# Last feed-forward stage of a two-block model on 256 columns instead of 272, with each input's high and low parts as one moving operand

## The chip, the cores and the metric

The kernel runs on one core of one Trainium2 chip. The metric is the device time of one execution in microseconds (us), the median of several runs. TensorE (PE in the rows) does the matmuls, VectorE is DVE, ScalarE is ACT, GpSimd is POOL, and SyncE (SP) issues the weight loads. PSUM is eight banks of 128 partitions by 512 fp32 values, named `bank0` to `bank7`.

## The reference, cut to what matters

Two blocks in a row. The first one puts 16 meta tokens ahead of 256 tokens and has two layers of feed-forward, mixer, feed-forward:

```python
h = jnp.concatenate([meta, x], axis=1)            # 16 + 256 rows of 1024
for l in range(DEPTH):                            # DEPTH = 2
    h = h + 0.5 * swiglu(rmsnorm(h, norm_gains[l, 0]), ...)
    h = h + mixer(rmsnorm(h, norm_gains[l, 1]), ...)
    h = h + 0.5 * swiglu(rmsnorm(h, norm_gains[l, 2]), ...)
return rmsnorm(h, final_norm)[:, N_META:]         # the 16 meta rows are dropped

def swiglu(x, w_gate, w_up, w_down):              # 1024 -> 2816 -> 1024
    return (jax.nn.silu(x @ w_gate) * (x @ w_up)) @ w_down
```

The second block (a short convolution, two mixtures of 64 experts, a sparse attention) works on the 256 tokens that are left. Everything is float32.

## The kernel before, in words

Activations lie transposed: features on the 128 partitions, rows of the sequence along the free dimension, the 256 tokens first and the 16 meta tokens behind them (`T` = 272, `SEQ` = 256). `H` is the residual in `KD` = 8 feature tiles. One stage is one of the reference's lines; the last feed-forward stage, `ffn(1, 1)`, is the subject here.

**Split products.** A feed-forward product is made of fp32r matmuls (a rounded form of fp32 that TensorE takes at one pass). Input and weights are each cut in a rounded high part and a rounded rest, the low part, and three products are summed in PSUM: low weights by high input, high weights by low input, high weights by high input. `split_sum` (matmuls at L528) does so for one *chunk* of weights, which is all `k` tiles of one 128-column output tile: 8 tiles for gate and up, 11 for half of a down product. `SQ` holds the input's high part and `XN` its low part; for the down products `HIDH` and `HID` (in `ARENA`) do.

**Who makes the parts.** The weights come by DMA into three ring buffers. ACT copies a chunk to its high part, rounded (`high_part`, L1057), and POOL subtracts that from the weights and leaves the low part (`low_parts`, L1758). High parts have room for `HIGHS` = 3 chunks, so `high_part` of chunk c waits until TensorE has finished chunk c - 3, and TensorE's chunk c waits for POOL's low part of it (`wl_ready`).

**The order of the work** is written out by hand for each engine, and each engine takes its instructions in that order. For each of the 22 hidden tiles `f`, TensorE makes chunk 2f (gate) in bank 0 or 2 and chunk 2f+1 (up) in bank 1 or 3; from f = 2 on it first waits for `hid_ready` of tile f - 2, which frees the banks. ACT does `Silu` of the gate bank into `SG` (L1097), and behind it the high parts of chunks 2f+3 and 2f+4:

```python
st.need(bank_full["act"][pair])
st.done(A(SG[:, f % 2, :], bank[pair][:, 0:T], ACT.Silu), silu_ready)
high_part()
high_part()
```

DVE waits for the silu and the up bank, multiplies them twice, once in fp32 (L1369) and once rounded into `HIDH` (L1370), and subtracts for the low part in `HID` (L1371, two inputs in SBUF), which gives `hid_ready`. Then come 16 down chunks in 8 banks; DVE adds half of each bank to `H` (L1376), and ACT squares `H` for the next norm (L1062). A norm is a matmul of the squares with a constant (L560), ACT's square root (L1072), DVE's reciprocal (L1328) and a chain of scaling (L1331), rounding (ACT, L1067) and subtracting (L1335). `then(...)` is an instruction of DVE and a wait for its own result.

The rows below also draw on two other stages with split products: the mixer's last part, where DVE does L1494 to L1499, and the convolution, where it does L1520 to L1529, both while POOL makes low parts. Lines L498 and L492 are the mixer's plain fp32 products, each of which leaves two records.

Of the kernel before, what the change touches and what calls it, by code (L numbers as in the profile page):

```python
# [7 lines left out]
ALU = mybir.AluOpType  # L8
# [6 lines left out]
P = 128  # L15
# [279 lines left out]
def build_model(nc, w, cst_dram, small_dram, h0_dram, table_dram, out_dram):  # L295
    CL, SL = const_layout(), small_layout()
    with ExitStack() as ctx:
        twins = {}

        def sb(name, shape, dt=F32, twin=False):  # L300
            if twin:
                with nc.sbuf_tensor(name + "_rounded", shape, F32R) as t:
                    twins[name] = t
            return ctx.enter_context(nc.sbuf_tensor(name, shape, dt))

        def rounded(view):
# [60 lines left out]
        sq_ready = sem("sq_ready")  # L367
        std_ready = sem("std_ready")
        xn_ready = sem("xn_ready")
        silu_ready = sem("silu_ready")  # L370
# [104 lines left out]
        def _(pe):  # L475
# [41 lines left out]
            def split_sum(o, tiles, start=True, stop=True, before=None, cols=slice(0, P), again=False):  # L517
# [12 lines left out]
                                               stop=(stop and k == len(tiles) - 1 and j == 2))  # L530
                return ins

            def chunk_done(ins, s):
# [13 lines left out]
            def rows(x, n=T):  # L547

                return [x[:, k, 0:n] for k in range(KD)]

            def pairs(high, low, n, m=T):

                return [(high[:, k, 0:m], low[:, k, 0:m]) for k in range(n)]

            def column_means(b, wgt, tiles, reader):

                claim(b)
                for k, x in enumerate(tiles):
# [5 lines left out]
            def rms_norm():  # L564
                column_means(7, "mean_d", rows(SQ), "act")

            def layer_norm(b):

# [8 lines left out]
                st.need(x_tile, KD)  # L577

            def ffn(l, j):
                rms_norm()  # L580
                tiles = pairs(SQ, XN, KD)
                for f in range(NF):
                    pair = 2 * (f % 2)
                    if f >= 2:
                        st.need(hid_ready)
                    for m, e in ((0, "act"), (1, "dve")):
                        claim(pair + m)
                        ins = split_sum(bank[pair + m][:, 0:T], tiles,
                                        before=(lambda k: st.need(xn_ready)) if f == 0 and m == 0 else None)
                        chunk_done(ins, bank_full[e][pair + m])  # L590
                tiles = pairs(HIDH, HID, NF)
                for c in range(4):
                    for h in range(2):
                        for dt in range(2):
                            b = (4 if c % 2 == 0 else 0) + dt
                            if h == 0:
                                claim(b)
                            last_hidden = lambda f: st.need(hid_ready) if f >= 9 else None
                            ins = split_sum(bank[b][:, 0:T], tiles[h * 11:h * 11 + 11], start=(h == 0), stop=(h == 1),
                                            before=last_hidden if (c, h, dt) == (0, 1, 0) else None)  # L600
# [415 lines left out]
            for l in range(2):  # L1016
                ffn(l, 0)
                mixer(l)
                ffn(l, 1)
            rms_norm()  # L1020
            convolution()
            layer_norm(0)
            experts(0)
# [8 lines left out]
        def _(act):  # L1032
# [41 lines left out]
            def rms_norm(first=False):  # L1074
                if first:
                    for k in range(KD):
                        square(k, True)
                deviation(RS[:, :], 7, "eps_rms", T, std_ready)

            def layer_norm(b):  # L1080
                st.need(d2a)
# [4 lines left out]
            def ffn(first=False, dense_next=False):  # L1086
                rms_norm(first)
                split_input(XN)
# [197 lines left out]
            for l in range(2):  # L1286
                ffn(first=(l == 0))
                mixer(l)
                ffn(dense_next=True)
            rms_norm()  # L1290
            convolution()
            layer_norm(0)
            experts(0)
# [8 lines left out]
        def _(dve):  # L1302
# [54 lines left out]
            def sum_from(b, k):  # L1357
# [2 lines left out]
                st.done(STT(R2[:, k, :], X2[:, k, :], ALPHA, bank[b][:, 0:SEQ], ALU.mult, ALU.add), sum_tile)  # L1360
                mark(bank_free["dve"][b])

            def ffn(l, j):
                normed_and_split("gains", (l * 3 + 2 * j) * KD, XN, xn_ready)
                for f in range(NF):
                    b = 2 * (f % 2) + 1
                    st.need(silu_ready)
                    st.need(bank_full["dve"][b])
                    st.done(TT(HID[:, f, :], SG[:, f % 2, :], bank[b][:, 0:T], ALU.mult))  # L1369
                    then(TT(rounded(HIDH[:, f, :]), SG[:, f % 2, :], bank[b][:, 0:T], ALU.mult))  # L1370
                    st.done(TT(rounded(HID[:, f, :]), HID[:, f, :], part(HIDH[:, f, :]), ALU.subtract), hid_ready)  # L1371
                for c in range(4):
                    for dt in range(2):
                        b, k = (4 if c % 2 == 0 else 0) + dt, 2 * c + dt
                        st.need(bank_full["dve"][b])
                        st.done(STT(H[:, k, :], bank[b][:, 0:T], 0.5, H[:, k, :], ALU.mult, ALU.add), h_tile)  # L1376
                        mark(bank_free["dve"][b])
# [538 lines left out]
```

## Time and profile before

| | us |
|---|---|
| median of 3 runs | 3162.02 |
| lowest and highest | 3161.73, 3163.46 |
| span of the profiled execution, first to last instruction | 3154.3 |
| what lies around the span, against the median | 7.7 |
| PE busy | 2718.0 (86%), 18120 matmul records |
| DVE, ACT, POOL busy | 920.7, 911.3, 890.8 (28 to 29% each) |
| split products of `ffn(1, 1)` on the chain | 197.03 |

The profile is of one execution, whose only time is its span. An engine's busy share is an average over all stages. What one stage is worth is read from the stage: from the rows of its own window, in order of time, and from what each engine waited for there.

### The profile page before, as it was taken

How to read it: one execution, taken by the hardware profiler on the slowest of the kernel's cores; microseconds unless marked ns; L12 is line 12 of the kernel's file. 1: busy time of each engine (PE TensorE's matmuls, PEld its weight loads, DVE VectorE, ACT ScalarE, POOL GpSimd, SP SyncE). 2: the span in 40 equal slices, each digit the busy share in tenths (PEclk: the TensorE clock that was granted, in tenths of full speed). 3: DMA queues.
4: the chain of work that ended last, by engine and by line, in shares of the span. 5: the costliest groups of instructions: out<-in, count | busy, mean ns of one | idle time of the engine just before them, and what ended most of it. 6: DMA issues, size and time to landing. Idle time of an engine off the chain costs nothing.

```text
span 3154.3 us, 44882 instructions
## 1 busy us (share of the span) xinstructions
PE 2718.0 (86%) x18120; PEld 2044.0 (65%) x18120; DVE 920.7 (29%) x2251; ACT 911.3 (29%) x1485; POOL 890.8 (28%) x374
## 2 busy tenths in 40 slices
PE   5999997899999999789987888888877769888886
PEld 3997666799999656789986433333366754334333
DVE  2211523521220243432164322222225343222222
ACT  3331361333433145133332111111124411111111
POOL 2882001578677001257863000000024500000000
PEclk8999996999999999699997899999978979999998
DMA  6543320354555322045455799999943169999994
GB/s 168 187 156 114 107 81 27 107 178 152 166 179 159 119 80 81 5 156 178 152 161 196 256 366 367 367 366 366 312 151 107 31 204 366 366 366 367 367 366 165
DMA packets 515163, 643.89 MB, mean 204 GB/s; under 512 B 16544, under 2 KB 450720, under 8 KB 514768
## 3 DMA queue, kind: packets, MB, share of 16 engines
q1 hardware_dynamic: 513424, 635.60, 60.2%
q0 software_dynamic: 1600, 6.29, 0.9%
q8 instruction: 104, 1.70, 0.2%
q14 instruction: 35, 0.29, 0.0%
HBM read 637.66 MB, written 4.19 MB: 203 GB/s over the span
## 4 chain that ended last, share of the span: by engine, by line
PE 62%; SPq 21%; DVE 8%; DMA 5%; issue 2%; ACT 2%; POOL 0%; DVEq 0%; ACTq 0%
PE bank L528 33%; PE bank L492 14%; SPq L1805 10%; SPq L1801 10%; DMA wring<-in_exp_w 4%; PE bank L983 3%; PE bank L778 2%; PE bank L944 2%; PE bank L968 1%; PE bank L560 1%; PE bank L695 1%; PE bank L957 1%; PE bank L502 1%; PE bank L991 1%; DMA bias_table<-ARENA 1%
## 5 line engine op out<-in xcount | busy, mean ns | idle before, releaser
L1758 POOL TENSOR_TENSOR wring_rounded<-wring,wring_rounded 128x1024 fp32r<-128x1024 f32 (+1 forms) x336 | 861.1, 2566 | 477.1 <-ACT wring_rounded L1057 454.1
L528 PE MATMUL bank<-SQ_rounded,wring_rounded 128*128 128x272 f32 (+1 forms) x3456 | 659.6, 291 | 45.0 <-POOL wring_rounded L1758 23.9
L528 PEld LDWEIGHTS bank<-SQ_rounded,wring_rounded 128*128 128x128 f32 x3456 | 550.6, 191 | 49.6 <-issue 38.4
L1057 ACT ACTIVATE wring_rounded<-wring 128x1024 fp32r<-128x1024 f32 (+1 forms) x336 | 375.1, 1119 | 489.9 <-PE bank L528 484.9
L528 PE MATMUL bank<-XN_rounded,wring_rounded 128*128 128x272 f32 (+1 forms) x1728 | 500.2, 289 | 0.0
L528 PE MATMUL bank<-ARENA_rounded,wring_rounded 128*128 128x272 f32 (+1 forms) x3456 | 447.8, 293 | 54.0 <-DVE ARENA_rounded L1489 27.6
L528 PEld LDWEIGHTS bank<-ARENA_rounded,wring_rounded 128*128 128x128 f32 x3456 | 444.9, 194 | 57.0 <-DVE ARENA_rounded L1489 28.5
L983 PE MATMUL bank<-wring,ARENA 128*32 128x512 f32 x2048 | 281.1, 672 | 139.1 <-DMA wring<-in_exp_w 108.8
L528 PEld LDWEIGHTS bank<-XN_rounded,wring_rounded 128*128 128x128 f32 x1728 | 331.7, 192 | 0.0
L1272 ACT ACTIVATE ARENA<-bank 128x512 f32<-128x512 f32 x128 | 76.4, 597 | 794.7 <-PE bank L983 794.7
L492 PE MATMUL bank<-XN,wring 128*128 128x272 f32 (+2 forms) x1088 | 257.1, 401 | 11.8 <-DVE XN L1342 11.8
L983 PEld LDWEIGHTS bank<-wring,ARENA 128*32 128x32 f32 x2048 | 57.5, 116 | 308.7 <-DMA wring<-in_exp_w 164.8
L968 PE MATMUL bank<-ARENA 64*128 64x512 f32 x1008 | 250.4, 615 | 0.0
L492 PEld LDWEIGHTS bank<-XN,wring 128*128 128x128 f32 (+2 forms) x1088 | 190.2, 180 | 68.1 <-DVE XN L1342 12.6
L991 PEld LDWEIGHTS bank<-CST,ARENA 128*128 128x128 f32 x1024 | 124.4, 192 | 117.2 <-ACT ARENA L1272 117.2
L1784 POOL DMA_DIRECT2D ARENA<-bias_table x8 | 6.0, 754 | 621.4 <-DVE H L1354 621.4
L1369 DVE TENSOR_TENSOR ARENA<-ARENA,bank 128x272 f32<-128x272 f32 x88 | 38.6, 438 | 430.8 <-PE bank L528 430.8
L944 PE MATMUL bank<-ARENA 128*128 128x128 f32 x1024 | 136.1, 288 | 32.0 <-DVE ARENA L1703 27.9
L1717 DVE TENSOR_TENSOR ARENA<-ARENA,bank 128x64 f32<-128x64 f32 x128 | 28.4, 222 | 462.4 <-ACT ARENA L1277 462.4
L944 PEld LDWEIGHTS bank<-ARENA 128*128 128x128 f32 x1024 | 123.5, 197 | 61.5 <-DVE ARENA L1703 34.2
L1767 POOL TENSOR_TENSOR ARENA_rounded<-ARENA,ARENA_rounded 128x256 fp32r<-128x256 f32 (+1 forms) x24 | 17.7, 737 | 498.6 <-ACTq L1039 498.6
L957 PE MATMUL bank<-ARENA 128*32 128x512 f32 x1024 | 143.2, 632 | 7.9 <-issue 7.9
(231 smaller groups left out, 2475.2 us busy)
## 6 DMA issues: line engine op xcount, KB each, us to landing
wring<-in_exp_w SPq DMA_DIRECT2D x256, 1024.0 KB, 11.7
ARENA<-in_exp_w SPq DMA_DIRECT2D x128, 1024.0 KB, 12.4
wring<-in_ffn_w_gate SPq DMA_DIRECT2D x44, 1024.0 KB, 5.3
wring<-in_ffn_w_up SPq DMA_DIRECT2D x44, 1024.0 KB, 7.9
wring<-in_ffn_w_down SPq DMA_DIRECT2D x32, 1408.0 KB, 6.3
wring<-in_w_in SPq DMA_DIRECT2D x16, 2048.0 KB, 7.7
wring<-in_conv_w_in SPq DMA_DIRECT2D x24, 512.0 KB, 5.4
wring<-in_attn_w_in SPq DMA_DIRECT2D x5, 2048.0 KB, 7.9
```

Source lines behind the costliest of these rows:

```text
L492: ins = nc.tensor.matmul(o, l, r, start=(i == 0), stop=(i == len(g) - 1))
L528: ins = nc.tensor.matmul(o, rounded(a_[:, k, cols]), rounded(x), start=(start and k == 0 and j == 0), stop=(stop and k == len(tiles) - 1 a ...
L944: ins = nc.tensor.matmul(GATHER[:, kk * P:(kk + 1) * P], XTOK[:, t, k * P:(k + 1) * P], GS[:, t, :], start=(t == 0), stop=(t == 1))
L957: ins = nc.tensor.matmul(DOWN[32 * q:32 * q + 32, :], HT[:, c * 32:c * 32 + 32], w2[:, c, dh * 512:dh * 512 + 512], start=True, stop=True, ...
L968: ins = nc.tensor.matmul(bank[2 * t + dh][:, :], PUT[64 * dh:64 * dh + 64, u % 2, t * P:(t + 1) * P], YS[64 * dh:64 * dh + 64, :], start=f ...
L983: ins = nc.tensor.matmul(UP[32 * q:32 * q + 32, :], XG[:, k, u * 32:u * 32 + 32], v[:, k, :], start=(k < 4), stop=(k >= 4), tile_position= ...
L991: ins = nc.tensor.matmul(TURN[:, f * 32:f * 32 + 32], HS[:, f * P:(f + 1) * P], const("sum4"), start=True, stop=True)
L1057: st.done(A(rounded(high), w_, ACT.Copy), wh_ready)
L1272: A(HS[:, :], UP[:, :], ACT.Copy).then_inc(m.hs, 1)
L1758: st.done(nc.gpsimd.tensor_tensor(rounded(low), low, part(high), ALU.subtract), wl_ready)
L1801: sp.dma_start(v[:, :, j, :], w[name][l][bass.ds(e, 1)].rearrange("o (k p) n -> p (o k) n", p=P)).then_inc(M[l].w13[u], 16)
L1805: sp.dma_start(W2B[:, u, :].rearrange("p (k n) -> p k n", k=2), w["exp_w2_2"][l][bass.ds(e, 1)].rearrange("o (k p) n -> p (o k) n", p=P)). ...
```

## The change

Only the stage `ffn(1, 1)` and the norm behind it change. They work on the 256 tokens alone. `XN` and `SQ` become the two halves of one tile `XS`, so that a moving operand of 2 x 256 columns can take the high part and the low part in one instruction. For each `k`, the new `wide_sum` issues two matmuls for the former three: the high weights by high and low input (512 columns, the whole bank), and the low weights by the high input (256 columns, onto the bank's first half). What was one sum of 272 columns is now two partial sums of 256 columns in one bank, and DVE adds them: for the gate ahead of the silu, which ACT then does in place on `SG`, for the up product ahead of the multiplication, and for the down product by adding both halves to `H` in turn.

```diff
+        def both(high, low):
+            ap = [list(x) for x in high.ap]
+            return bass.AP(tensor=twins[high.tensor.name], offset=high.offset,
+                           ap=[ap[0], [low.offset - high.offset, 2], ap[1]])
...
-        XN = sb("XN", [P, KD, T], twin=True)
-        SQ = sb("SQ", [P, KD, T], twin=True)
+        XS = sb("XS", [P, 2, KD, T], twin=True)
+        SQ, XN = XS[:, 0], XS[:, 1]
...
+            def wide_sum(o, tiles, start=True, stop=True, before=None):
...
+                pe.wait_ge(wl_ready, c + 1)
+                for k, (xh, xl) in enumerate(tiles):
+                    if before:
+                        before(k)
+                    nc.tensor.matmul(o[:, 0:2 * SEQ], rounded(high[:, k, :]), both(xh, xl),
+                                     start=(start and k == 0), stop=False, skip_group_check=True)
+                    ins = nc.tensor.matmul(o[:, 0:SEQ], rounded(low[:, k, :]), rounded(xh),
+                                           start=False, stop=(stop and k == len(tiles) - 1), skip_group_check=True)
...
-                    for m, e in ((0, "act"), (1, "dve")):
+                    for m, e in ((0, "act" if n == T else "dve"), (1, "dve")):
...
-                    st.need(bank_full["act"][pair])
-                    st.done(A(SG[:, f % 2, :], bank[pair][:, 0:T], ACT.Silu), silu_ready)
+                    if n == T:
+                        st.need(bank_full["act"][pair])
+                        st.done(A(SG[:, f % 2, :], bank[pair][:, 0:T], ACT.Silu), silu_ready)
+                    else:
+                        st.need(gate_ready)
+                        st.done(A(SG[:, f % 2, 0:n], SG[:, f % 2, 0:n], ACT.Silu), silu_ready)
...
+            def ffn_of_tokens(gain, at):
+                normed_and_split(gain, at, XN, xn_ready, SEQ)
+                for f in range(NF):
+                    g, u = bank[2 * (f % 2)], bank[2 * (f % 2) + 1]
+                    sg, hid, high = SG[:, f % 2, 0:SEQ], HID[:, f, 0:SEQ], HIDH[:, f, 0:SEQ]
+                    st.need(bank_full["dve"][2 * (f % 2)])
+                    then(v.tensor_copy(sg, g[:, 0:SEQ]))
+                    st.done(TT(sg, sg, g[:, SEQ:2 * SEQ], ALU.add), gate_ready)
+                    st.need(bank_full["dve"][2 * (f % 2) + 1])
+                    then(v.tensor_copy(hid, u[:, 0:SEQ]))
+                    then(TT(hid, hid, u[:, SEQ:2 * SEQ], ALU.add))
+                    st.need(silu_ready)
+                    st.done(TT(hid, sg, hid, ALU.mult))
+                    st.settle()
+                    then(v.tensor_copy(rounded(high), hid))
+                    st.done(TT(rounded(hid), hid, part(high), ALU.subtract), hid_ready)
+                for c in range(4):
+                    for dt in range(2):
...
+                        then(STT(h, bank[b][:, 0:SEQ], 0.5, h, ALU.mult, ALU.add))
+                        st.done(STT(h, bank[b][:, SEQ:2 * SEQ], 0.5, h, ALU.mult, ALU.add), h_tile)
+                        mark(bank_free["dve"][b])
```

What DVE does for two hidden tiles of this stage, before (L1369 to L1371, three instructions a tile):

```order
L1369 TENSOR_TENSOR ARENA<-ARENA,bank 128x272
L1370 TENSOR_TENSOR ARENA_rounded<-ARENA,bank 128x272
L1371 TENSOR_TENSOR ARENA_rounded<-ARENA,ARENA_rounded 128x272
L1369 TENSOR_TENSOR ARENA<-ARENA,bank 128x272
L1370 TENSOR_TENSOR ARENA_rounded<-ARENA,bank 128x272
L1371 TENSOR_TENSOR ARENA_rounded<-ARENA,ARENA_rounded 128x272
```

and in the changed kernel, for one hidden tile and the start of the next:

```order
L1398 COPY ARENA<-bank 128x256
L1399 TENSOR_TENSOR ARENA<-ARENA,bank 128x256
L1401 COPY ARENA<-bank 128x256
L1402 TENSOR_TENSOR ARENA<-ARENA,bank 128x256
L1404 TENSOR_TENSOR ARENA<-ARENA 128x256
L1406 CAST ARENA_rounded<-ARENA 128x256
L1407 TENSOR_TENSOR ARENA_rounded<-ARENA,ARENA_rounded 128x256
L1398 COPY ARENA<-bank 128x256
```

Three instructions of a tile have become seven. One of the old three read SBUF alone; of the new seven the last three do. The sum of the next gate (L1398, L1399) stands behind them.

What ACT does for one hidden tile and the start of the next, from f = 2 on, with the semaphores that each waits for; before:

```order
L1097 ACTIVATE ARENA<-bank 128x272 [waits bank0_full_act,hid_ready]
L1057 ACTIVATE wring_rounded<-wring 128x1024 [waits bank0_full_act,w_ready0]
L1057 ACTIVATE wring_rounded<-wring 128x1024 [waits bank1_full_dve,w_ready1]
L1097 ACTIVATE ARENA<-bank 128x272 [waits bank2_full_act,hid_ready]
L1057 ACTIVATE wring_rounded<-wring 128x1024 [waits bank2_full_act,w_ready1]
```

and in the changed kernel:

```order
L1125 ACTIVATE ARENA<-ARENA 128x256 [waits gate_sum_ready,hid_ready]
L1081 ACTIVATE wring_rounded<-wring 128x1024 [waits bank0_full_dve,w_ready0]
L1081 ACTIVATE wring_rounded<-wring 128x1024 [waits bank1_full_dve,w_ready1]
L1125 ACTIVATE ARENA<-ARENA 128x256 [waits gate_sum_ready,hid_ready]
L1081 ACTIVATE wring_rounded<-wring 128x1024 [waits bank2_full_dve,w_ready1]
```

The silu waited for TensorE's gate bank; it now waits for DVE's sum of the gate, and the two high parts stand behind it as before.

## Rows read from the trace of the kernel before

**Rows 1.** The page's chain that ended last, by engine
```profile
PE 62%; SPq 21%; DVE 8%; DMA 5%; issue 2%; ACT 2%; POOL 0%; DVEq 0%; ACTq 0%
```

**Rows 2.** The same chain in order of time: start, us, what
```profile
1386.56 197.03 PE bank L528 x1566
1583.59 3.68 PE bank L560 x16
```

**Rows 3.** Two stretches: PE, PEld, DVE, ACT, POOL busy, clock, DMA share, GB/s
```profile
1386.50:1518.50 132.00, 131.94 (x1051) 131.78 (x1052) 27.50 (x68) 55.36 (x68) 104.33 (x43) 1.00 0.48 150
1518.50:1583.50 65.00, 65.00 (x518) 65.00 (x517) 4.02 (x8) 22.04 (x22) 50.74 (x17) 1.00 0.61 182
```

**Rows 4.** Timeline of one hidden tile of `ffn(1, 1)`: start, us, instruction, idle before
```profile
1451.02 1.06 ACT L1057 ACTIVATE wring_rounded<-wring 128x1024 fp32r<-128x1024 f32 x1 [1.66 <-PE bank L528]
1451.03 0.44 DVE L1369 TENSOR_TENSOR ARENA<-ARENA,bank 128x272 f32<-128x272 f32 x1 [4.75 <-PE bank L528]
1451.85 0.44 DVE L1371 TENSOR_TENSOR ARENA_rounded<-ARENA,ARENA_rounded 128x272 fp32r<-128x272 f32 x1
1452.15 2.40 POOL L1758 TENSOR_TENSOR wring_rounded<-wring,wring_rounded 128x1024 fp32r<-128x1024 f32 x1 [0.32 <-ACT wring_rounded L1057]
1454.02 0.40 ACT L1097 ACTIVATE ARENA<-bank 128x272 f32<-128x272 f32 x1 [1.95 <-PE bank L528]
1454.32 1.05 ACT L1057 ACTIVATE wring_rounded<-wring 128x1024 fp32r<-128x1024 f32 x1
1455.44 2.41 POOL L1758 TENSOR_TENSOR wring_rounded<-wring,wring_rounded 128x1024 fp32r<-128x1024 f32 x1 [0.89 <-ACT wring_rounded L1057]
1457.04 0.44 DVE L1369 TENSOR_TENSOR ARENA<-ARENA,bank 128x272 f32<-128x272 f32 x1 [4.75 <-PE bank L528]
```

**Rows 5.** Timeline of the down chunks of the same stage, POOL
```profile
1543.57 3.22 POOL L1758 TENSOR_TENSOR wring_rounded<-wring,wring_rounded 128x1408 fp32r<-128x1408 f32 x1 [0.93 <-ACT wring_rounded L1057]
1547.73 3.22 POOL L1758 TENSOR_TENSOR wring_rounded<-wring,wring_rounded 128x1408 fp32r<-128x1408 f32 x1 [0.94 <-ACT wring_rounded L1057]
```

**Rows 6.** Timeline of other products: convolution, its output product, fp32 of 272 columns
```profile
1602.05 0.40 PE L528 MATMUL bank<-SQ_rounded,wring_rounded 128*128 128x256 f32 x2
1602.40 0.40 PE L528 MATMUL bank<-SQ_rounded,wring_rounded 128*128 128x256 f32 x2
...
1680.94 2.41 POOL L1758 TENSOR_TENSOR wring_rounded<-wring,wring_rounded 128x1024 fp32r<-128x1024 f32 x1 [0.29 <-ACT wring_rounded L1057]
1683.67 2.41 POOL L1758 TENSOR_TENSOR wring_rounded<-wring,wring_rounded 128x1024 fp32r<-128x1024 f32 x1 [0.31 <-ACT wring_rounded L1057]
...
310.76 0.40 ACT L1126 ACTIVATE SQ<-bank 128x272 f32<-128x272 f32 x1 [3.27 <-PE bank L492]
314.43 0.40 ACT L1126 ACTIVATE SQ<-bank 128x272 f32<-128x272 f32 x1 [3.27 <-PE bank L492]
```

**Rows 7.** Timeline of the mixer's last part: DVE beside POOL
```profile
1318.10 0.45 DVE L1499 TENSOR_TENSOR ARENA_rounded<-ARENA,ARENA_rounded 128x272 fp32r<-128x272 f32 x1
1318.27 2.53 POOL L1758 TENSOR_TENSOR wring_rounded<-wring,wring_rounded 128x1024 fp32r<-128x1024 f32 x1 [0.83 <-ACT wring_rounded L1057]
1318.81 0.43 DVE L1496 TENSOR_TENSOR ARENA<-ARENA,bank 128x272 f32<-128x272 f32 x1
1319.28 1.81 DVE L1497 TENSOR_TENSOR ARENA<-ARENA 128x272 f32<-128x272 f32 x1
1321.12 0.30 DVE L1498 CAST ARENA_rounded<-ARENA 128x272 fp32r<-128x272 f32 x1
```

**Rows 8.** Timeline of the convolution: a DVE instruction with one SBUF tensor beside POOL
```profile
1603.00 4.81 POOL L1758 TENSOR_TENSOR wring_rounded<-wring,wring_rounded 128x1024 fp32r<-128x1024 f32 x2 [15.83 <-ACT wring_rounded L1057]
...
1604.82 0.73 DVE L1523 TENSOR_SCALAR ARENA<-ARENA,SM 128x256 f32<-128x256 f32 x1 [0.18 <-DVE ARENA L1520]
```

**Rows 9.** Instruction groups of the attention: DVE copies out of PSUM, busy and mean ns
```profile
L1449 DVE COPY ARENA<-bank 128x256 f32<-128x256 f32 x16 | 6.6, 412 | 2.8 <-PE bank L502 2.8
```

**Rows 10.** A stretch of the mixer's last part: PE busy, clock, DMA share, GB/s
```profile
1325.00:1330.00 5.00, 2.23 (x11) 0.78 0.00 0
```

More of the change, by code:

```diff
@@ L369, in build_model @@
         xn_ready = sem("xn_ready")
-        silu_ready = sem("silu_ready")
+        silu_ready, gate_ready = sem("silu_ready"), sem("gate_sum_ready")
         hid_ready = sem("hid_ready")
@@ L531, in split_sum @@
                 return ins
+            def wide_sum(o, tiles, start=True, stop=True, before=None):
+                progress["chunk"] += 1
+                c = progress["chunk"] - 1
+                low, high = chunk_views(c)
+                pe.wait_ge(wl_ready, c + 1)
[6 more added lines that the diff above has]
+                                           start=False, stop=(stop and k == len(tiles) - 1), skip_group_check=True)
+                return ins
             def chunk_done(ins, s):
@@ L562, in column_means, with rms_norm @@
                 st.done(ins, bank_full[reader][b])
-            def rms_norm():
-                column_means(7, "mean_d", rows(SQ), "act")
+            def rms_norm(n=T):
+                column_means(7, "mean_d", rows(SQ, n), "act")
             def layer_norm(b):
@@ L579, in ffn @@
             def ffn(l, j):
-                rms_norm()
-                tiles = pairs(SQ, XN, KD)
+                n = SEQ if (l, j) == (1, 1) else T
+                total = wide_sum if n == SEQ else split_sum
+                rms_norm(n)
+                tiles = pairs(SQ, XN, KD, n)
                 for f in range(NF):
@@ L585, in ffn @@
                         st.need(hid_ready)
-                    for m, e in ((0, "act"), (1, "dve")):
+                    for m, e in ((0, "act" if n == T else "dve"), (1, "dve")):
                         claim(pair + m)
-                        ins = split_sum(bank[pair + m][:, 0:T], tiles,
-                                        before=(lambda k: st.need(xn_ready)) if f == 0 and m == 0 else None)
+                        ins = total(bank[pair + m][:, 0:2 * SEQ if n == SEQ else T], tiles,
+                                    before=(lambda k: st.need(xn_ready)) if f == 0 and m == 0 else None)
                         chunk_done(ins, bank_full[e][pair + m])
-                tiles = pairs(HIDH, HID, NF)
+                tiles = pairs(HIDH, HID, NF, n)
                 for c in range(4):
@@ L598, in ffn @@
                             last_hidden = lambda f: st.need(hid_ready) if f >= 9 else None
-                            ins = split_sum(bank[b][:, 0:T], tiles[h * 11:h * 11 + 11], start=(h == 0), stop=(h == 1),
-                                            before=last_hidden if (c, h, dt) == (0, 1, 0) else None)
+                            ins = total(bank[b][:, 0:2 * SEQ if n == SEQ else T], tiles[h * 11:h * 11 + 11],
+                                        start=(h == 0), stop=(h == 1),
+                                        before=last_hidden if (c, h, dt) == (0, 1, 0) else None)
                             if h == 1:
@@ L1019, in _ @@
                 ffn(l, 1)
-            rms_norm()
+            rms_norm(SEQ)
             convolution()
@@ L1072, in deviation, with rms_norm @@
                 st.done(A(out, bank[b][:, 0:n], ACT.Sqrt, bias=const(eps)), s)
-            def rms_norm(first=False):
+            def rms_norm(first=False, n=T):
                 if first:
@@ L1077, in rms_norm @@
                         square(k, True)
-                deviation(RS[:, :], 7, "eps_rms", T, std_ready)
+                deviation(RS[:, 0:n], 7, "eps_rms", n, std_ready)
             def layer_norm(b):
@@ L1084, in layer_norm, with ffn @@
                 deviation(RS[:, 0:SEQ], b + 1, "eps_ln", SEQ, std_ready)
-            def ffn(first=False, dense_next=False):
-                rms_norm(first)
-                split_input(XN)
+            def ffn(first=False, dense_next=False, n=T):
+                rms_norm(first, n)
+                split_input(XN, n)
                 if first:
@@ L1288, in _ @@
                 mixer(l)
-                ffn(dense_next=True)
-            rms_norm()
+                ffn(dense_next=True, n=SEQ if l == 1 else T)
+            rms_norm(n=SEQ)
             convolution()
@@ L1361, in sum_from @@
                 mark(bank_free["dve"][b])
+            def ffn_of_tokens(gain, at):
[16 more added lines that the diff above has]
+                    for dt in range(2):
+                        b, k = (4 if c % 2 == 0 else 0) + dt, 2 * c + dt
+                        h = H[:, k, 0:SEQ]
+                        st.need(bank_full["dve"][b])
+                        then(STT(h, bank[b][:, 0:SEQ], 0.5, h, ALU.mult, ALU.add))
+                        st.done(STT(h, bank[b][:, SEQ:2 * SEQ], 0.5, h, ALU.mult, ALU.add), h_tile)
+                        mark(bank_free["dve"][b])
             def ffn(l, j):
+                if (l, j) == (1, 1):
+                    ffn_of_tokens("gains", (l * 3 + 2 * j) * KD)
+                    return
                 normed_and_split("gains", (l * 3 + 2 * j) * KD, XN, xn_ready)
```

## The prediction

> **What bounds the kernel now.** I read the chain of waits first: TensorE holds 62% of it, DVE 8%, POOL next to nothing [rows 1]. In order of time, the split products of the last feed-forward stage are one piece of 197.03 us in which TensorE waits for nothing, and the mean of the next norm follows at once [rows 2]. The stretches of the stage say the same: PE busy throughout at full clock, ACT under half busy, DVE a fifth, but POOL 104.33 of 132 us while gate and up are made and 50.74 of 65 in the down part [rows 3]. So the stage is bound by the pace of its matmuls, and POOL is the engine with the least room.
>
> A hidden tile takes 6.01 us, the distance of two L1369 [rows 4], for 48 matmuls: 125.2 ns each, 113.3 of them for 272 columns at 2.4 GHz. A down chunk takes 4.16 us for 33 [rows 5]: 126 ns. The columns are nearly the whole price.
>
> **What the matmuls save.** Three times 272 columns (816) become 512 + 256 (768), and three weight loads two. What comes on top of the columns differs: 12 ns a matmul in this stage; 12 in the convolution, where three matmuls of 256 columns take 0.35 to 0.36 us against 0.32 of columns; 7 in its output product, where 24 take 2.73 us, 113.5 each [rows 6]. No fp32r matmul of 512 columns is in the trace. The nearest long one is a plain fp32 record of 272 columns: 3.67 us for 16, 229 ns each, 226.7 of them two passes over the columns [rows 6], so 2.5 on top. Bounds for a pair: 320 ns of columns + 2.5 + 12 = 335 if the excess shrinks for the long one, and 356 if it is a share of the columns (11%). I take 345, 12 for each load, near the middle. The saving is 31 ns a pair. Gate and up have 22 x 2 x 8 = 352 pairs (a chunk 3.01 -> 2.76 us), down has 16 x 11 = 176 (4.16 -> 3.80). TensorE alone would save 11 + 5.8 us.
>
> The TensorE page of the Trainium skill ("Back-to-back issue gap") gives 2.5 ns over the columns per matmul, so 325 ns a pair, an estimate from that page; the rows of this stage disagree with it at 12 ns for the short ones and agree for the long one.
>
> **What DVE gets.** Seven instructions a tile for three. Copy from PSUM 0.41 us [rows 9], additions with a PSUM operand 0.43 [rows 7], some 0.04 between dependent ones (0.42 for 256 columns). Gate sum 0.87, up sum 0.91 with its wait, product 0.42, cast 0.29, subtraction 0.42: about 3 us of 5.5. By length that fits. By its neighbours it may not.
>
> **The wait that appears.** In the mixer, L1497 (both inputs in SBUF) takes 1.81 us instead of 0.44 and ends 0.29 after POOL's L1758; L1496, with a PSUM input, takes 0.43 in the middle of the same POOL instruction; and a POOL instruction that starts 0.17 after L1499 takes 2.53 instead of 2.40 [rows 7]. So a DVE instruction on SBUF alone and POOL's subtraction exclude each other: whoever starts first runs, the other waits. POOL lets go some 0.14 before its record ends, DVE 0.28 after its start. L1523, with a single SBUF tensor, also waits for the first of two POOL instructions (0.73 us) [rows 8]. Before, a hidden tile had one such instruction, and L1371 fell into POOL's pause from 1451.83 to 1452.15 [rows 4]. Now it has three, product, cast and subtraction, and POOL's two take 4.8 of 5.5 us. They must meet.
>
> The cast is the open one: L1498 took 0.30, but no POOL instruction was running [rows 7]. The SBUF page of the Trainium skill ("Who interferes with whom") says that copies and casts between SBUF can also take the pair of ports that DVE shares with GpSimd. No run so far shows it for the cast; L1523 is the nearest row, and I let the cast wait as it does.
>
> **What is queued behind it.** DVE's gate sum of f+1 stands behind the subtraction of f; ACT's silu waits for that sum; behind the silu stands the high part of chunk 2f+5, the up chunk of f+2; POOL waits for it, TensorE for POOL. Going round this loop with the durations above, every second tile is hit fully:
> - TensorE up(f): 2.76
> - up sum on DVE: 0.99 with the hand-over; the POOL instruction that began 0.26 before the up chunk's end lets go at 2.00, and the product ends at 2.42
> - POOL's next instruction was queued and has the port before the cast asks: the cast ends 2.41 later
> - subtraction: 0.46; altogether 5.29 from the up chunk
> - gate sum f+1: 0.80; silu: 0.43; high part with hand-over: 1.03 [rows 4]
> - POOL 2.40, hand-over 0.07, and TensorE may start up(f+2).
>
> That is 12.78 us for two tiles: 6.39 each against 6.01, although TensorE needs 5.52. It stands idle 1.74 us once in two tiles. In the odd tile product and cast slip through and only the subtraction waits. A pair price of 335 or 356 moves this by nothing, since the up chunk then starts when POOL says. If the cast does not wait, it takes 0.33 for 2.41, but the subtraction is then caught, 2.2 for 0.46: 5.0 for 5.29, and the two tiles take 12.45, 6.23 each.
>
> **The sum.** Gate and up: the first two tiles run on the three chunks made ahead at 5.5 (-1.0), twenty at +0.38 (+7.6): +6.6. Entry to the down part: the second down chunk's high part stands behind the last silu, which comes 1.8 after the last up chunk (its gate sum stands behind a subtraction that POOL held up); 1.35 for the high part and 3.4 for the low one make 6.6, and TensorE ends the first down chunk at 3.8: it waits 2.8, where it waited 0. Down: 16 x 0.36 = -5.8; POOL's 3.22 and ACT's 1.38 stay under 3.80, and DVE's second addition to `H` reads PSUM and excludes nobody. Edges: two means on 256 columns, 3.68 -> 3.5 us each [rows 2], and a norm chain of some 8.5 us on a seventeenth fewer columns: -0.8 (bounds 0 and -1). The second addition of the last bank (+0.44) lies beside ACT's high part of 1.06 and costs nothing there. The second mean, 3.68 us long, covers it. Loads: the 150 GB/s of gate and up stay about as they are and the down part's 182 become 200 [rows 3]; TensorE never waited for them and the buffers are three deep, so no cost. Sum: 6.6 + 2.8 - 5.8 - 0.8 = **+2.8 us**: a span of 3157.1, and a median of 3164.8, since the median stands 7.7 above the span. By bounds: pair 335, cast free: -2.6; pair 356, POOL holding to its record's end (+0.2 a tile): +9.
>
> A measurement of this kernel can tell some 0.2%, 6.3 us, from no change. So I forecast no change that can be told: TensorE's saving is real and is handed to the port.
>
> **Rivals.**
> 1. *Exclusion does not bite.* DVE's three fall into pauses as L1371 does, or PE's pace keeps the engines in step. For it: before, all of it fell in step, for 22 tiles. Against: 0.7 us of pause a tile cannot hold three instructions and their waits. It would give -11 - 5.8 - 0.8 = -17.6: 3144.4. Chance 0.13. With half of the tiles in step: 3151 to 3156, chance 0.08.
> 2. *One blocked wait more in the loop* (the slower side). If the product of the odd tile is also caught, or the hand-overs are 0.1 us longer, so that POOL's queued instruction wins once more, two tiles cost 2.4 more: 15.2. Over ten double tiles +24: 3189; for half of them 3177. It decides when the odd up sum ends after POOL's start instead of 0.6 before it, and that is a margin of half a microsecond. Chance 0.15.
> 3. *The clock falls.* TensorE is idle 1.74 us in 12.8. In the mixer a stretch with over half idle shows 0.78 [rows 10], a mix of the 1.2 and 2.4 GHz levels. Here the busy share is 86%, so I do not expect it; once a loop would cost about 1 us of matmul each: +10, 3175. Chance 0.06.
> 4. *The pairs cost what the triples did* (376 ns; a long moving operand of two pieces costs extra, or the excess grows). Gate and up go by POOL and DVE, down saves nothing: 3171. Chance 0.05.
>
> **Chances and range.** The forecast (0.53) spans -2.6 to +9, of it 0.45 within 6.3 us and 0.07 above, 0.01 below. Faster: 0.13 + 0.07 of rival 1 + 0.01 = 0.21. Slower: 0.07 + 0.15 + 0.06 + 0.05 = 0.33. Same: 0.46. The range from 3150 to 3182 takes in the half-in-step case, the clock, the dear pairs and half of rival 2, and leaves out some 0.2; the likeliest case's own is 3159 to 3171.
>
> **What would show it.** In the changed kernel's timeline of one hidden tile: products, casts or subtractions of 1.5 to 2.5 us that end 0.3 behind POOL's record; TensorE waiting for POOL or its queue once in two tiles, and pieces of the chain of waits that name POOL, ACT and DVE where there were none; a gate and up stretch of 137 to 141 us and a down stretch near 62. Down chunks at 3.68 or 3.92 us would correct the pair price. I am wrong if gate and up run at 5.5 us a tile, or if the casts always take 0.29 with POOL running.

## The result, and the profile after

Over 20 runs each, the changed kernel takes 3168.09 us (median; 3161.24 to 3170.53) and the kernel before 3163.44 (3156.56 to 3166.55). The ratio is 1.0015, with a 95% interval of 1.0008 to 1.0022: 4.7 us slower, 2.5 to 7.0 by the interval. That is no change by the 0.2% of the prediction, but the interval leaves out zero: over 20 runs each it is a small loss.

The two profiled spans differ by more, 3154.3 and 3164.4. The norm's mean ahead of the stage and the one behind it frame the part that was changed. The chain of the kernel before, in order of time (start, us, what):

```profile
1374.10 3.95 PE bank L560 x16
...
1583.59 3.68 PE bank L560 x16
```

and of the changed kernel:

```profile
1380.66 3.73 PE bank L581 x16
...
1594.31 0.24 PE bank L548
1595.01 3.47 PE bank L581 x16
```

From mean to mean it is 209.5 us before and 214.4 after: 4.9 more, close to the measured 4.7. Of the 10.1 us between the spans another 6.6 are there when the stage begins, in code that the change leaves alone, and 1.3 come back behind it. Nor is the profiled execution of the kernel before a typical one. Wherever a time and its span are both on record, the time is 1.8 or 1.9 us above the span; so by my estimate the execution with the span of 3154.3 took about 3156.1, some 6 us less than the median of before. I compare stages by the distance from mean to mean from here on, since it is free of that.

The new waits of the changed kernel, from the stage's window (engine, line, who was waited for: us in total, times, longest):

```profile
ACT ARENA L1125 <- DVE ARENA L1399: 80.3, 22, 5.3
POOL wring_rounded L1815 <- ACT wring_rounded L1081: 51.4, 23, 12.5
DVE ARENA L1401 <- PE bank L550: 23.0, 11, 2.1
PE bank L548 <- POOL wring_rounded L1815: 15.9, 11, 2.4
```

Before, TensorE waited for nothing in 197 us [rows 2]. Now it waits 11 times for POOL, 15.9 us in all: ten times once in two hidden tiles, 1.3 to 1.4 us each, and 2.4 us at the entry to the down part. And the silu waits for DVE's gate sum 22 times. DVE's own instructions say why (busy, mean ns, idle before):

```profile
L1407 DVE TENSOR_TENSOR ARENA_rounded<-ARENA,ARENA_rounded 128x256 fp32r<-128x256 f32 x22 | 30.8, 1401 | 0.8
L1406 DVE CAST ARENA_rounded<-ARENA 128x256 fp32r<-128x256 f32 x22 | 30.2, 1372 | 0.8
L1404 DVE TENSOR_TENSOR ARENA<-ARENA 128x256 f32<-128x256 f32 x22 | 18.2, 826 | 0.8
L1402 DVE TENSOR_TENSOR ARENA<-ARENA,bank 128x256 f32<-128x256 f32 x22 | 9.3, 422 | 0.8
```

The three that touch SBUF alone take 1401, 1372 and 826 ns on average, where their lengths are 420, 300 and 420; the one with a PSUM operand takes its 422. Those are 54 us of waiting that the record counts as busy.

One turn of the loop, two hidden tiles, from the timeline of the changed kernel:

```profile
1434.69 4.94 POOL L1815 TENSOR_TENSOR wring_rounded<-wring,wring_rounded 128x1024 fp32r<-128x1024 f32 x2
1436.17 1.20 DVE L1404 TENSOR_TENSOR ARENA<-ARENA 128x256 f32<-128x256 f32 x1
1437.40 2.37 DVE L1406 CAST ARENA_rounded<-ARENA 128x256 fp32r<-128x256 f32 x1
1439.81 0.43 DVE L1407 TENSOR_TENSOR ARENA_rounded<-ARENA,ARENA_rounded 128x256 fp32r<-128x256 f32 x1
1440.15 0.42 DVE L1398 COPY ARENA<-bank 128x256 f32<-128x256 f32 x1
1440.60 0.42 DVE L1399 TENSOR_TENSOR ARENA<-ARENA,bank 128x256 f32<-128x256 f32 x1
1441.11 0.42 ACT L1125 ACTIVATE ARENA<-ARENA 128x256 f32<-128x256 f32 x1 [4.74 <-DVE ARENA L1399]
1441.44 2.00 ACT L1081 ACTIVATE wring_rounded<-wring 128x1024 fp32r<-128x1024 f32 x2
1441.85 0.43 DVE L1404 TENSOR_TENSOR ARENA<-ARENA 128x256 f32<-128x256 f32 x1
1442.31 0.30 DVE L1406 CAST ARENA_rounded<-ARENA 128x256 fp32r<-128x256 f32 x1
1442.56 9.94 POOL L1815 TENSOR_TENSOR wring_rounded<-wring,wring_rounded 128x1024 fp32r<-128x1024 f32 x4 [2.94 <-ACT wring_rounded L1081]
1442.64 2.58 DVE L1407 TENSOR_TENSOR ARENA_rounded<-ARENA,ARENA_rounded 128x256 fp32r<-128x256 f32 x1
...
1449.02 1.22 DVE L1404 TENSOR_TENSOR ARENA<-ARENA 128x256 f32<-128x256 f32 x1
```

In the first tile the product waits for POOL's running instruction (1.20), the cast for its next one (2.37). Behind them stand the gate sum (L1398, L1399), the silu, two high parts, and POOL, which stood idle for 2.94 us meanwhile. In the second tile product and cast slip through (0.43, 0.30), the subtraction does not (2.58). POOL is held up by DVE too, for less: its 44 instructions of this length take 2.40 us on average before and 2.48 now; the pair of 4.94 us is one of 2.40 and one of 2.57, which starts while the product has not ended. The turn takes 1449.02 - 1436.17 = 12.85 us, 6.43 a tile, against 6.01 before [rows 4].

The price of the pair, first while the hidden tiles are made (TensorE's records) and then in the down part (DVE's first reading of a finished bank; one down chunk lies between the two):

```profile
1448.61 0.40 PE L548 MATMUL bank<-XS_rounded,wring_rounded 128*128 128x512 f32 x1
1448.84 0.28 PE L550 MATMUL bank<-XS_rounded,wring_rounded 128*128 128x256 f32 x1
1448.96 0.40 PE L548 MATMUL bank<-XS_rounded,wring_rounded 128*128 128x512 f32 x1
...
1450.72 0.40 PE L548 MATMUL bank<-XS_rounded,wring_rounded 128*128 128x512 f32 x1
```

```profile
1545.14 0.42 DVE L1413 SCALAR_TENSOR_TENSOR H<-bank,H 128x256 f32<-128x256 f32 x1 [11.13 <-PE bank L550]
...
1548.99 0.42 DVE L1413 SCALAR_TENSOR_TENSOR H<-bank,H 128x256 f32<-128x256 f32 x1 [2.96 <-PE bank L550]
```

Six pairs from 1448.61 to 1450.72 are 352 ns each; eleven in 3.85 us are 350. A down chunk took 4.16 before [rows 5].

### The profile page after: what moved, and what is told of

It is laid out like the page before. It is cut to its first block, busy times and chain, and to the rows that moved or that the text cites. A ratio compares the mean times of both kernels' runs of the same rounds, so it can differ in the third digit from the quotient of the medians.

```text
span 3164.4 us, 43922 instructions
## 1 busy us (share of the span) xinstructions
PE 2709.5 (86%) x17592; PEld 2007.0 (63%) x17592; DVE 1008.6 (32%) x2347; ACT 910.6 (29%) x1485; POOL 892.4 (28%) x374
## 4 chain that ended last, share of the span: by engine, by line
PE 60%; SPq 18%; DVE 10%; DMA 6%; ACT 2%; issue 2%; POOL 1%; DVEq 0%; ACTq 0%
PE bank L534 27%; PE bank L498 14%; SPq L1862 9%; SPq L1858 9%; DMA wring<-in_exp_w 5%; PE bank L1007 3%; PE bank L548 2%; PE bank L968 2%; PE bank L802 2%; PE bank L992 2%; PE bank L581 1%; PE bank L981 1%; PE bank L719 1%; PE bank L508 1%; POOL wring_rounded L1815 1%
## 5 line engine op out<-in xcount | busy, mean ns | idle before, releaser
L534 PE MATMUL bank<-XS_rounded,wring_rounded 128*128 128x272 f32 (+1 forms) x4128 | 524.6, 290 | 41.8 <-POOL wring_rounded L1815 24.9
L534 PEld LDWEIGHTS bank<-XS_rounded,wring_rounded 128*128 128x128 f32 x4128 | 522.4, 192 | 45.2 <-issue 35.0
L534 PE MATMUL bank<-ARENA_rounded,wring_rounded 128*128 128x272 f32 (+1 forms) x2928 | 381.5, 294 | 55.6 <-DVE ARENA_rounded L1546 27.3
L534 PEld LDWEIGHTS bank<-ARENA_rounded,wring_rounded 128*128 128x128 f32 x2928 | 378.9, 195 | 58.7 <-DVE ARENA_rounded L1546 28.5
L498 PE MATMUL bank<-XS,wring 128*128 128x272 f32 (+2 forms) x1088 | 259.2, 404 | 11.8 <-DVE XS L1370 11.8
L498 PEld LDWEIGHTS bank<-XS,wring 128*128 128x128 f32 (+2 forms) x1088 | 191.0, 181 | 69.5 <-DVE XS L1370 12.6
L548 PE MATMUL bank<-XS_rounded,wring_rounded 128*128 128x512 f32 x352 | 127.6, 404 | 17.5 <-POOL wring_rounded L1815 13.5
L1015 PE MATMUL bank<-CST,ARENA 128*128 128x32 f32 x1024 | 138.0, 279 | 1.4 <-ACT ARENA L1300 1.4
L1426 DVE TENSOR_TENSOR ARENA<-ARENA,bank 128x272 f32<-128x272 f32 x66 | 28.9, 438 | 327.7 <-PE bank L534 327.7
```

The source lines that it names most:

```text
L498: ins = nc.tensor.matmul(o, l, r, start=(i == 0), stop=(i == len(g) - 1))
L534: ins = nc.tensor.matmul(o, rounded(a_[:, k, cols]), rounded(x), start=(start and k == 0 and j == 0), stop=(stop and k == len(tiles) - 1 a ...
L548: nc.tensor.matmul(o[:, 0:2 * SEQ], rounded(high[:, k, :]), both(xh, xl), start=(start and k == 0), stop=False, skip_group_check=True)
L1015: ins = nc.tensor.matmul(TURN[:, f * 32:f * 32 + 32], HS[:, f * P:(f + 1) * P], const("sum4"), start=True, stop=True)
```

## The experiments

The theory: the saving of TensorE is real, and is lost to a loop (product, cast and subtraction held up by POOL; gate sum behind them; silu; high part; POOL; TensorE). The rivals: that the port is simply full; that seven instructions of DVE are too long a chain; that the pairs cost about what the triples did.

**e1: cut the loop, leave the waits.** ACT makes one high part ahead of the silu and of the wait for `hid_ready` (cut to this stage; the other stages keep their order):

```diff
-                    if f >= 2:
+                    if f >= 2 and n == T:
                         st.need(hid_ready)
...
+                        high_part()
+                        if f >= 2:
+                            st.need(hid_ready)
                         st.need(gate_ready)
                         st.done(A(SG[:, f % 2, 0:n], SG[:, f % 2, 0:n], ACT.Silu), silu_ready)
-                    high_part()
+                    if n == T:
+                        high_part()
                     high_part()
```

> The changed kernel with one edit: ACT makes the high part of chunk 2f+3 ahead of the silu of tile f, not behind it; all arithmetic, all DVE instructions and all three waits for the port stay. Loop theory (the loss is the loop DVE sum, silu, high part, POOL, TensorE): the loop is cut, the pauses of TensorE go, a hidden tile takes 8 x 2 x 352 ns = 5.63 us, gate and up plus down take 22 x 5.63 + 16 x 3.85 = 186 us for 199 before, and with the shorter norms the kernel is some 14 us faster than before (ratio 0.9955). Capacity rival (POOL's 4.8 us and DVE's three port instructions of 0.3 do not fit in 5.63 us whatever the order): the tile stays near 6.2 to 6.4 and the kernel within 6 us of before or slower. DVE-length rival (seven instructions are too long a chain by themselves): no change against the changed kernel, ratio 1.0015.

Measured: 3145.01 us, ratio 0.9945 (0.9932 to 0.9959). From mean to mean it is 195.5 us, 14.0 less than before, and once its hidden tiles have begun TensorE waits for nobody. By the ratio the whole kernel is 17 us faster (13 to 21). The stage's 14.0 lie inside that; the rest lies outside the stage, in code that the edit leaves alone, and its cause stays open. DVE's groups in the stage, and the timeline of one tile:

```profile
L1410 DVE CAST ARENA_rounded<-ARENA 128x256 fp32r<-128x256 f32 x22 | 50.9, 2315 | 0.8
L1411 DVE TENSOR_TENSOR ARENA_rounded<-ARENA,ARENA_rounded 128x256 fp32r<-128x256 f32 x22 | 12.3, 558 | 0.8
L1408 DVE TENSOR_TENSOR ARENA<-ARENA 128x256 f32<-128x256 f32 x22 | 10.7, 487 | 0.8
```

```profile
1438.57 0.43 DVE L1408 TENSOR_TENSOR ARENA<-ARENA 128x256 f32<-128x256 f32 x1
1438.85 2.40 POOL L1819 TENSOR_TENSOR wring_rounded<-wring,wring_rounded 128x1024 fp32r<-128x1024 f32 x1 [0.35 <-ACT wring_rounded L1081]
1439.03 2.37 DVE L1410 CAST ARENA_rounded<-ARENA 128x256 fp32r<-128x256 f32 x1
...
1444.20 0.43 DVE L1408 TENSOR_TENSOR ARENA<-ARENA 128x256 f32<-128x256 f32 x1
```

A tile takes 1444.20 - 1438.57 = 5.63 us, TensorE's pace. The cast still waits, and takes 2315 ns on average for its 300: 49 us of waiting by the three groups, nearly the 54 of the changed kernel, and it costs nothing. So there is room for POOL's and DVE's work in 5.63 us (the capacity rival falls), the chain is not too long, and the pairs are cheaper than the triples. It was the order in which the waits stood.

**e2: leave the loop, take the waits away.** The silu goes to PSUM, and a second product takes the place of the cast:

```diff
-                        st.done(A(SG[:, f % 2, 0:n], SG[:, f % 2, 0:n], ACT.Silu), silu_ready)
+                        st.done(A(bank[6 + f % 2][:, 0:n], SG[:, f % 2, 0:n], ACT.Silu), silu_ready)
...
-                    st.done(TT(hid, sg, hid, ALU.mult))
-                    st.settle()
-                    then(v.tensor_copy(rounded(high), hid))
+                    act_sg = bank[6 + f % 2][:, 0:SEQ]
+                    st.done(TT(rounded(high), act_sg, hid, ALU.mult))
+                    then(TT(hid, act_sg, hid, ALU.mult))
```

> The changed kernel with the silu written to PSUM banks 6 and 7, so that both products read one operand there (a second product takes the place of the cast, as in the kernel before): still seven DVE instructions a tile, of the same lengths or longer (product 0.42 for cast 0.29), but only the subtraction needs the port. Exclusion theory: products take 0.42 us also beside POOL, at most one wait a tile remains, TensorE's pauses go, a tile takes 5.63 us and the kernel is some 14 us faster than before (0.9955). DVE-length rival: nothing changes or it gets 0.1 us a tile worse, ratio 1.0015 to 1.002.

Measured: 3145.49 us, ratio 0.9945 (0.9932 to 0.9959); 195.1 us from mean to mean. The products in its trace, with an operand in PSUM:

```profile
L1407 DVE TENSOR_TENSOR ARENA_rounded<-ARENA,ARENA_rounded 128x256 fp32r<-128x256 f32 x22 | 14.6, 662 | 0.7
L1405 DVE TENSOR_TENSOR ARENA_rounded<-bank,ARENA 128x256 fp32r<-128x256 f32 x22 | 9.3, 424 | 0.7
L1406 DVE TENSOR_TENSOR ARENA<-bank,ARENA 128x256 f32<-128x256 f32 x22 | 9.1, 415 | 0.0
```

424 and 415 ns, with POOL running beside them; only the subtraction still waits, 0.24 us on average. A tile takes 5.60 us. Seven instructions and the old order of ACT are harmless without the waits: the length rival falls. POOL's own work in the loop is as long as before here (2.49 us on average), so it was DVE's waits that made the loop too long.

**e3: shorten what is waited for.** POOL makes two of the 8 or 11 weight tiles of a low part in this stage, and the matmuls use those two in turn, so most of the low weights are left out:

```diff
                     pool.wait_ge(wh_ready, c + 1)
+                    if chunks[c][0][0] in ("up", "down") and chunks[c][0][1:3] == (1, 1):
+                        low, high = low[:, 0:2, :], high[:, 0:2, :]
...
-                    ins = nc.tensor.matmul(o[:, 0:SEQ], rounded(low[:, k, :]), rounded(xh),
+                    ins = nc.tensor.matmul(o[:, 0:SEQ], rounded(low[:, k % 2, :]), rounded(xh),
```

> The changed kernel in which POOL makes only the first two of 8 (or 11) weight tiles of each low part of the last feed-forward stage (0.6 to 0.75 us instead of 2.4 and 3.2), and the matmuls with the low weights use those two in turn: it leaves out most of the low weights. DVE's and ACT's work and order are unchanged. Exclusion theory: no wait above 0.7 us is left, a tile takes 5.63 us, kernel some 14 us faster than before (0.9955). DVE-length rival: as the changed kernel, 1.0015.

Measured: 3144.03 us, ratio 0.9943 (0.9929 to 0.9957); 194.9 us from mean to mean. POOL and the cast beside it, from the timeline:

```profile
1438.72 0.73 POOL L1817 TENSOR_TENSOR wring_rounded<-wring,wring_rounded 128x256 fp32r<-128x256 f32 x1 [0.84 <-ACT wring_rounded L1081]
1438.89 0.71 DVE L1406 CAST ARENA_rounded<-ARENA 128x256 fp32r<-128x256 f32 x1
```

The cast's time follows POOL's: 0.71 us beside 0.73, where it was 2.37 beside 2.40. Order and number of DVE's and ACT's instructions are those of the changed kernel. By itself this run does not part DVE's waits from POOL's own share of the loop, since both shrink with POOL's instruction; e2 does.

**e4: the 256 columns without the joined operand.** The kernel before with n = 256 in this stage, three matmuls for each k (two of its places):

```diff
-                        ins = split_sum(bank[pair + m][:, 0:T], tiles,
+                        ins = split_sum(bank[pair + m][:, 0:n], tiles,
...
-                    st.done(TT(HID[:, f, :], SG[:, f % 2, :], bank[b][:, 0:T], ALU.mult))
+                    st.done(TT(HID[:, f, 0:n], SG[:, f % 2, 0:n], bank[b][:, 0:n], ALU.mult))
```

> The kernel before with 256 columns for 272 in the last feed-forward stage and its norms, three matmuls for each k as before, no joined operand, DVE's old three instructions. Column theory (price is columns plus 12 ns, as the convolution's triple of 357 ns shows): a tile takes 16 x 357 = 5.71 us, a down chunk 3.93 us; 22 x 0.30 + 16 x 0.23 = 10.3 saved, with the norms 11 us faster than before (0.9965). If the excess of this stage does not fall with its columns, 376 ns a triple: only the norms' 0.8 us, ratio 0.9998. If it is at 357, dropping 16 columns gives nearly all that the joined operand (352 ns a pair in the changed kernel's trace) gives.

Measured: 3152.08 us, ratio 0.9969 (0.9958 to 0.9979). The chain:

```profile
1376.99 3.73 PE bank L560 x16
1385.22 189.97 PE bank L528 x1581
1575.20 3.47 PE bank L560 x16
```

198.2 us from mean to mean, 11.3 less than before: the column theory's 11. A tile takes 5.71 us, so a triple costs 357 ns and a pair 351: by the stage's distance, of the 14.0 us of e1 the sixteen columns bring 11 and the joined operand 3. The medians of the two kernels are 7.1 us apart. Of their profiled executions 4.1 us lie behind the second mean, in code that is alike in both: from there to the span's end it is 3150.2 - 1575.20 = 1575.0 us in e4 and 3143.1 - 1572.24 = 1570.9 in e1. So the joined operand's 3 us are read from the stage, and the medians alone would give it too much.

**e5, e6, e7: why a pair costs 351 and not 335.** All three on the kernel of e1. e5 gives the wide matmul one contiguous piece as its moving operand (the high weights; the product with the input is left out), e6 takes the low weights' matmul first, e7 lays the hidden tiles 256 columns apart:

```diff
-                    nc.tensor.matmul(o[:, 0:2 * SEQ], rounded(high[:, k, :]), both(xh, xl),
+                    nc.tensor.matmul(o[:, 0:2 * SEQ], rounded(high[:, k, :]), rounded(high[:, 0:4, :]),
```

```diff
+                    if not first:
+                        nc.tensor.matmul(o[:, 0:SEQ], rounded(low[:, k, :]), rounded(xh),
+                                         start=False, stop=False, skip_group_check=True)
+                    ins = nc.tensor.matmul(o[:, 0:2 * SEQ], rounded(high[:, k, :]), both(xh, xl),
```

```diff
+        HIDS, HIDHS = Arena(0)(NF, SEQ), Arena(a.n)(NF, SEQ)
...
-                    sg, hid, high = SG[:, f % 2, 0:SEQ], HID[:, f, 0:SEQ], HIDH[:, f, 0:SEQ]
+                    sg, hid, high = SG[:, f % 2, 0:SEQ], HIDS[:, f, :], HIDHS[:, f, :]
```

> Price of the pair, on the kernel of e1 (where TensorE sets the pace, so that the distance of two tiles is the price). The 512-column matmul takes one contiguous piece of 512 columns (the high weights themselves) as moving operand instead of two pieces of 256 columns of the input: it leaves out the high weights' product with the input. Two-pieces theory (the pair costs 351 ns and not 335 since the operand jumps): 351 falls to about 340, a tile to 5.45 us, a down chunk from 3.85 to 3.74. Share-of-columns theory (some 10% on top of all columns of this kernel's split products): no change, 5.62 and 3.85.

> On the kernel of e1: for each k but the first, the 256-column matmul with the low weights goes ahead of the 512-column one. Same work, same results up to the order of the sum. If the excess comes from a weight load that is waited for behind the short matmul, the order is as good as before and nothing changes, since loads and matmuls still take turns: 5.62 us a tile. It would change by more than 0.05 us only if the price hangs on which bank half is written last or on the distance between the two uses of the same moving columns.

> On the kernel of e1: the hidden tiles and their high parts lie at a distance of 256 columns instead of 272, as the moving operands of the convolution's output product do, which has 7 ns on top of its columns instead of 12. If the distance is what makes that difference, a down chunk takes 11 x (320 + 2 x 7) = 3.67 us instead of 3.85, 2.8 us less over the stage, and gate and up stay at 5.62 a tile; the kernel is then 17 us faster than before by the stage's own lengths, ratio 0.9936. If the distance is nothing, a down chunk stays at 3.85 and the kernel as e1, 0.9945.

Measured: from mean to mean 194.7, 194.9 and 195.6 us, against 195.5 of e1. A tile takes 5.57, 5.60 and 5.60 us for 5.63, and a down chunk, over four in a row, 3.86, 3.83 and 3.89 for 3.84. The kernel of e8 below, whose stage is that of e1, also has 5.60 us a tile and 195.0 from mean to mean, so that much is the difference of two executions. None of the three moves the price by more than 2%: the two-pieces theory wanted 5.45 and 3.74 of e5, the distance theory 3.67 of e7, whose down part goes the wrong way. e7's median is 3145.49 us, ratio 0.9945 (0.9932 to 0.9959), as e1. e5 and e6 ran once each (3139.89 and 3144.46 us), and these two times decide nothing.

**e8: the same cure elsewhere.** e1, and in both mixers' last part the sum reads PSUM and the cast goes:

```diff
-                    then(TT(GB[:, k, :], GB[:, k, :], bank[b + 1][:, 0:T], ALU.mult), bank_free["dve"][b + 1])
-                    then(TT(GA[:, k, :], GA[:, k, :], GB[:, k, :], ALU.add))
-                    then(v.tensor_copy(rounded(GAH[:, k, :]), GA[:, k, :]))
+                    then(TT(bank[b + 1][:, 0:T], GB[:, k, :], bank[b + 1][:, 0:T], ALU.mult))
+                    st.done(TT(rounded(GAH[:, k, :]), GA[:, k, :], bank[b + 1][:, 0:T], ALU.add))
+                    then(TT(GA[:, k, :], GA[:, k, :], bank[b + 1][:, 0:T], ALU.add), bank_free["dve"][b + 1])
```

> The kernel of e1, with e2's means carried to the last part of both mixers: the product of the gate and the bank is written back to PSUM, both sums (rounded and not) read it there, and the cast goes, so that of three DVE instructions a tile that need the port one is left. In e1's trace these three waited 13.1 us in the first mixer and 12.9 us in the second over their lengths of 0.44 and 0.30, on a chain that TensorE waits for. Exclusion theory: the sums no longer wait; the subtraction may still be caught by 2.4 us in some tiles, so 5 to 20 us less than e1 in all, most likely 12: ratio to before about 0.991. If DVE's waits there are covered by TensorE or the weights, ratio as e1, 0.9945.

Measured: 3130.26 us, ratio 0.9893 (0.9877 to 0.9910): 34 us faster than before, some 15 to 17 less than e1, inside the 5 to 20 expected and above the likeliest 12. The sum, rounded and not, in e8's second mixer, over the same sum in e1's:

```profile
L1558 DVE TENSOR_TENSOR ARENA_rounded<-ARENA,bank 128x272 fp32r<-128x272 f32 x8 | 3.5, 437 | 0.3
L1559 DVE TENSOR_TENSOR ARENA<-ARENA,bank 128x272 f32<-128x272 f32 x8 | 3.4, 429 | 0.0
```

```profile
L1558 DVE TENSOR_TENSOR ARENA<-ARENA 128x272 f32<-128x272 f32 x8 | 8.1, 1008 | 0.3
```

437 and 429 ns where it was 1008. The subtraction still waits there (1262 ns on average in e8), so something is left. The two sums of e8 take some 12 us less of DVE's time over both mixers than e1's sum and cast did, while the time from the mean ahead of a mixer to the mean behind it falls by 9.7 and 7.5 us; where the other 5 to 6 come from is not shown.

## Why the prediction was right, point by point

- **No change that can be told, by +2.8 us.** Measured +4.7 by the ratio and +4.9 by the stage, inside the likeliest case and the range; with 20 runs each it can be told after all. In parts: from the mean to the first gate matmul -0.4 us; from there to the first down matmul 134.8 us before (1382.07 to 1516.90) and 142.5 now (1388.26 to 1530.79), +7.7 for the forecast +6.6, and just over the 137 to 141 that I wrote; the down part with its entry -2.5 for -3.0.
- **A term that was misnamed.** The 7.7 us between the span of before and the median are not what lies around a span. That is 1.8 to 1.9; the rest is that the profiled execution was a quick one. It does no harm, since the sum adds a difference to the median of before either way.
- **The wait that appears, and its loop.** Forecast 12.78 us for two tiles, 12.85 found; product and cast caught in one tile, the subtraction in the other, TensorE idle once in two tiles: as written. The parts: cast 2.41 forecast, 2.37 found; POOL's 2.40, found 2.37 to 2.41 for some and 2.57 to 2.60 for those that start beside one of DVE's three, which the forecast did not have.
- **The cast** was the open step, and it waits. By this case's own rows that is now shown (2.37 us beside POOL, 0.71 beside a short POOL instruction, 0.30 alone), and it agrees with what the page "SBUF — State Buffer" of the Trainium skill says of casts ("Who interferes with whom").
- **The pair.** "I take 345" was low: 352 and 350, near the upper bound of 356, the value for an excess that is a share of the columns. It changes the down part by 16 x 0.05 = 0.8 us and little else, because the loop sets the pace elsewhere. The 325 ns that the prediction worked out from "TensorE: Matmul & The Clock Gate" of the Trainium skill is further off.
- **Entry to the down part.** 2.8 us forecast, 2.4 found.
- **A reason that was wrong.** Against rival 1 I wrote that 0.7 us of pause a tile cannot hold three instructions and their waits. In e1 it does: 5.63 us a tile, with 2.2 us of DVE's time spent waiting. POOL loses some 0.05 us a tile to DVE there, and DVE's waiting is free as long as nobody needed for POOL's next chunk stands behind it. So the saving was not lost to the port as such, as "handed to the port" says, but to what stood behind it.
- **The rivals.** Rival 1 (3144.4) did not happen, but its time is what e1 to e3 reach: 3145.0, 3145.5, 3144.0. That they agree so closely is luck: rival 1 has -17.6 us for the stage, and e1 gains 14.0 there, since its 528 pairs cost 351 ns and not 345; the rest of its time comes from outside the stage. One more blocked wait in the loop, and the dear pairs, did not happen. The clock granted from 1386.5 to 1518.5 is 0.99, against 1.00 [rows 3], and it is 0.99 in e1 too, so it did not fall to any effect.

## What to carry to other kernels

In every stage read here, DVE instructions that touch only SBUF and GpSimd's subtraction on SBUF exclude each other for a whole instruction: beside a GpSimd instruction of 2.4 us, 0.30 and 0.43 us become up to 2.4 and 2.6, while instructions with an operand in PSUM keep their 0.42. That costs nothing where nobody stands behind the wait; so before adding such an instruction, ask what is queued behind it, and whether that leads back to GpSimd. If it does, either let one operand lie in PSUM (e2, e8), or let the work that feeds GpSimd go ahead of what waits for DVE (e1).

When a change has two parts, time the plain one alone: 256 columns for 272 gave 11 of the 14 us to be had in the stage, with none of the new waits.

## What the runs showed of the hardware that I had not expected

- The fp32r matmuls of this stage cost about 10% over their columns, long or short: over the 352 pairs of gate and up in e1, the next matmul starts 235 ns after one of 512 columns (213 at 2.4 GHz) and 117 after one of 256 (107), on average; while plain fp32 records of 272 columns had 2.5 ns on top [rows 6]. One piece or two, the order of the two, and the distance of the rows (e5 to e7) do not explain it; it stays open what does.
- A CAST of 256 columns with one operand, 0.30 us long, waits out a GpSimd instruction of 2.40 us like one with two SBUF operands does. It ends 0.15 us behind GpSimd's record (e1: 1441.40 for 1441.25), the longer product and subtraction 0.28 behind it.
- The time of a record can be nearly all waiting: 50.9 us of "busy" casts in e1 are 6.6 us of work.
